# Two transformer blocks on one core: split weights in slots 4224 bytes apart, tiles of six projections moved 112 bytes in

## The chip, the cores and the metric

The kernel runs on one NeuronCore of a Trainium2 chip. The metric is the device time of one execution in microseconds (us). The clock granted to TensorE is 1.00 of its full 2.4 GHz in all stretches that are shown.

## The reference

Two blocks are applied to 256 tokens of width 2048, all in fp32. The first has a mixer of two attentions (one over 8 heads with a top-64 selection through an indexer, one over 8 heads with a gate), a cross-attention to 256 memory tokens and a SwiGLU of width 5632. The second has an adaptive modulation, an mLSTM in both directions beside a Fourier mixing, and a gated feed-forward with a convolution over the tokens. Cut to the products that matter here:

```python
proj = x @ w_in                      # q_dsa, c_kv, q_idx, k_idx, w_idx, q_m, k_m, v_m, ga, gb
o = jnp.einsum('shc,hcd->shd', o_lat, w_uv)
merged = g_a * (o_a @ w_o_dsa) + g_b * (o_b @ w_o_moba); y = merged @ w_out
k, v = jnp.split(mem @ w_kv, 2, axis=-1)
g, u = jnp.split(x @ w_in, 2, axis=-1); y = (silu(g) * u) @ w_out
p = h @ w_in                         # u_f (fourier), q, k, v, o_gate, gates
x = x + gate1[:, None, :] * (mix @ w_out)
u = depthwise_conv_centred(h2 @ w_up, w_conv, b_conv); x = x + gate2[:, None, :] * ((silu(a) * v) @ w_down)
```

## The kernel before, in words

All weights come from memory in one stream of tiles of 128 x 2048 fp32 (1 MB each), in the order of the table TILES, through four buffers `raw`. Each tile has two halves of 1024 columns. To keep fp32 accuracy with the fast format fp32r, each half is split: ScalarE copies it, rounded, to a slot of `whi` (line 633), and VectorE writes the difference `raw - whi` to the slot of `wlo` of the same number (line 1249). There are four slots in each, used in turn (`h % 4` for half h). Tokens are split in the same way: `xhi`, `xlo` (the normed input of a projection), `ohi`, `olo` (attention outputs), `mhi`, `mlo` (memory), `shi`, `slo`, `dhi`, `dlo` (sources of the wide products). A product is three matmuls: upper by upper, upper by lower, lower by upper.

A matmul on this engine first loads a block of 128 columns into the array (PEld in the profile), and then streams the other operand through it (PE). The kernel has three kinds:

- Kind (a), form "T" in `product` (line 2215): a 128x128 block of weights is loaded, and 256 tokens are streamed. The output has its features on the partitions. It serves most projections: q_idx, w_uk, qk, gate_a, gates, k_mem, q_mem, up1, lstm_q, lstm_gates, lstm_k, lstm_o, up2.
- Kind (b), in `wide_tile` (line 2258) and the turns before and after it (lines 2283, 2305): 128 tokens are loaded, 512 columns of weights are streamed. It serves out1, o_mem, down1, out2, down2.
- Kind (c), form "N" in `product` (line 2219): the same shape as (b), for the six projections whose result is wanted with tokens on the partitions: latent (three blocks of 336 columns to a half), v_moba, w_uv, v_mem, lstm_v and fourier (two blocks of 512 columns to a half).

The places in SBUF are given out by hand, in bytes of a partition. `raw` begins at 16,512, `whi` at 49,280, `wlo` at 65,664, `xhi` at 82,048, `xlo` at 98,688. The tokens do not begin at the start of `xhi` and `xlo`: the table SKEW moves them in by 112 bytes, and `behind()` puts those in `ohi`, `olo`, `mhi`, `mlo`, `ckhi` and `cklo` 16 bytes ahead of a multiple of 128, which is the same place modulo 128. Modulo 1024, `xhi`, `ohi`, `olo`, `mhi`, `mlo` begin at 240 and `xlo` at 496. The sources of the wide products, `shi`, `slo`, `dhi` and `dlo`, begin at 128 modulo 1024, and so does each slot of `whi` and `wlo`.

The order of the work on each engine is written out in the program. It is set by semaphores: TensorE waits for `lo_ready` ahead of each half tile, ScalarE for `weights_used` ahead of each slot that it writes again.

Of the kernel before, what the change touches and what calls it, by code (L numbers as in the profile page):

```python
# [6 lines left out]
F32 = mybir.dt.float32  # L7
F32R = mybir.dt.float32r
BF16 = mybir.dt.bfloat16
I32 = mybir.dt.int32  # L10
ALU = mybir.AluOpType
ACT = mybir.ActivationFunctionType
AX_X = mybir.AxisListType.X

P = 128
# [27 lines left out]
SKEW = [(112,)] * 6  # L43
# [13 lines left out]
def blocks_of(x, n, b):  # L57
# [5 lines left out]
TILES = [("latent", 3), ("q_idx", 8), ("v_moba", 8), ("w_uk", 1), ("w_uv", 1),  # L63
         ("qk", 24), ("gate_a", 16), ("gates", 32), ("out1", 16), ("k_mem", 4), ("q_mem", 4), ("v_mem", 4), ("o_mem", 4), ("up1", 8 * FC), ("down1", FT),
         ("lstm_q", 4), ("lstm_gates", 1), ("lstm_k", 4), ("lstm_v", 8), ("lstm_o", 8), ("fourier", 8), ("out2", 16),
         ("up2", 8 * FC), ("down2", FT)]
# [20 lines left out]
AT, G = starts(TILES)  # L87
# [8 lines left out]
FEW = LATENT + IDX_DIM + IDX_HEADS  # L96
BLOCKS = [(0, 0, 0, 256, 0), (0, 1, 128, 256, 256), (1, 0, 0, 128, 384), (1, 1, 0, 256, 512)]


class Order:  # L100


# [23 lines left out]
def two_blocks(nc, x, xt, memt, stream, w_ada, cols, ln_cols, rows, ln_g, ln_b, norm_f, c_row, gate_bias, dft, out, max_store, gate_store):  # L126
    with ExitStack() as ctx:
# [5 lines left out]
        def sb(name, shape, dt=F32, offset=None):  # L133

            here = place[0] if offset is None else offset
            if offset is None:
                size = int(np.prod(shape[1:])) * (2 if dt == BF16 else 4)
                place[0] += -(-size // 32) * 32
            return nc.alloc_sbuf_tensor_at(name, shape, dt, offset=here)


        raw = [sb(f"raw{s}", [P, D]) for s in range(4)]
        whi = sb("whi", [P, 4, 1024], F32R)
        wlo = sb("wlo", [P, 4, 1024], F32R)
        at_shi = place[0]
        at_xhi = place[0]
        xhi = sb("xhi", [P, KT * S + 128 // 4], F32R)
# [66 lines left out]
        at_end = place[0]  # L214
        place[0] += 4096
        ident = sb("ident", [P, P])
        ones = sb("ones", [P, P])
        warm = sb("warm", [P, P], BF16)
        dist = sb("dist", [P, 384])
        causal = sb("causal", [P, 384])  # L220
# [107 lines left out]
        hi_ready = sem("hi_ready")  # L328
        lo_ready = sem("lo_ready")
# [280 lines left out]
        def _(act):  # L610
# [8 lines left out]
            def upper(g, i=None, per=0, halves=(0, 1), slot_of=None):  # L619

                if g >= G:
                    return
                for half in halves:
                    h = 2 * g + half
                    if g < 3 and half == 0 and i is None:
                        act.wait_ge(first_half_landed[g], 16)
                    elif g < 3 or half == 0:
                        act.wait_ge(raw_landed[g % 4], at(16 * (g // 4 + 1), i, 4 * per))
                    if slot_of is not None:
                        act.wait_ge(weights_used, 2 * slot_of + half + 1)  # L630
                    elif h >= 4:
                        act.wait_ge(weights_used, at(h - 3, i, 2 * per))
                    act.activation(whi[:, h % 4], raw[g % 4][:, 1024 * half:1024 * half + 1024], ACT.Copy)\  # L633
                       .then_inc(hi_ready, 1)

            def x_first_upper(b):
# [66 lines left out]
            def second_upper_of_next(g):  # L703

                act.wait_ge(weights_used, 2 * (g - 4) + 5)
                act.activation(whi[:, (2 * g + 1) % 4], raw[g % 4][:, 1024:2048], ACT.Copy).then_inc(hi_ready, 1)

            def first_uppers(n, scale, shift):

# [53 lines left out]
            g0 = AT["latent"]  # L763
            def first_tile_upper(k):

                return act.activation(whi[:, 0, FEW * k:FEW * k + FEW], raw[0][:, FEW * k:FEW * k + FEW], ACT.Copy)

            x_first_upper(0)
            act.wait_ge(first_half_landed[0], 16)
# [37 lines left out]
            for n in range(8):  # L807
                g = AT["v_moba"] + n
# [10 lines left out]
            g = AT["w_uk"]  # L819
# [3 lines left out]
            g = AT["w_uv"]  # L823
# [13 lines left out]
            for head in range(HEADS):  # L837
                g, q = g0 + 2 * head, head % 4
# [31 lines left out]
            with act.Fori(0, 2) as i:  # L870
                for unit in range(2):
                    g, c = g0 + 8 * unit, c0 + 3 * unit
# [52 lines left out]
            def last_turn(name, src, n0, hi=shi):  # L925

                last = AT[name] + SIZE[name] - 1

                def source(s):

                    act.activation(hi[:, s], src[:, 4 * n0 + s], ACT.Copy).then_inc(shi_ready, 1)

                def half_of_more(s, half):

                    g = last - 3 + s
                    act.wait_ge(raw_landed[g % 4], 16 * (g // 4 + 1))
                    return act.activation(more_hi[name][:, 2 * (s - 1) + half], raw[g % 4][:, 1024 * half:1024 * half + 1024], ACT.Copy)

                def half_of_last(half):

                    act.wait_ge(raw_landed[last % 4], 16 * (last // 4 + 1))
                    act.wait_ge(weights_used, 2 * (last - 4) + half + 1)
                    return act.activation(whi[:, (2 * last + half) % 4], raw[last % 4][:, 1024 * half:1024 * half + 1024], ACT.Copy)

                source(0)
                if name == "down1":
                    act.wait_ge(ada_used, ADA)
                half_of_more(1, 0).then_inc(ahead_hi, 1)
                source(1)
                half_of_more(2, 0).then_inc(ahead_hi, 1)  # L950
                source(2)
                half_of_last(0).then_inc(ahead_hi, 1)
                act.wait_ge(weights_used, through(last - 4))
                source(3)
                half_of_more(1, 1).then_inc(hi_ready, 2)
                half_of_more(2, 1).then_inc(hi_ready, 2)
                half_of_last(1).then_inc(hi_ready, 2)
# [163 lines left out]
            for n in range(4):  # L1121
                name = "lstm_o" if n < 2 else "fourier"
# [116 lines left out]
        def _(dve):  # L1239
            order = Order(dve, dve_order)  # L1240

            def rest(g, i=None, per=0, halves=(0, 1)):

                if g >= G:
                    return
                for half in halves:
                    h = 2 * g + half
                    dve.wait_ge(hi_ready, at(h + 1, i, 2 * per))
                    dve.tensor_tensor(wlo[:, h % 4], raw[g % 4][:, 1024 * half:1024 * half + 1024], whi[:, h % 4].bitcast(F32),  # L1249
                                      ALU.subtract).then_inc(lo_ready, 1)  # L1250

            def x_first_rest(b):

# [62 lines left out]
            g0, wide_n = AT["latent"], LATENT + IDX_DIM + IDX_HEADS  # L1316
            def first_tile_rest(k):

                return dve.tensor_tensor(wlo[:, 0, FEW * k:FEW * k + FEW], raw[0][:, FEW * k:FEW * k + FEW],
                                         whi[:, 0, FEW * k:FEW * k + FEW].bitcast(F32), ALU.subtract)  # L1320

            x_first_rest(0)
            dve.wait_ge(first_tile_hi, 1)
# [123 lines left out]
            with dve.Fori(0, 2) as i:  # L1447
                order.enter(i, 24)
                for q in range(4):
                    g = g0 + 2 * q  # L1450
# [73 lines left out]
            def last_turn(name, src, n0, hi=shi, lo=slo):  # L1524

                last = AT[name] + SIZE[name] - 1
                turns_before = 3 * ("down1", "out2", "down2").index(name)

                def source(s):

                    dve.wait_ge(shi_ready, SRC[name] + 4 * n0 + s + 1)
                    dve.tensor_tensor(lo[:, s], src[:, 4 * n0 + s], hi[:, s].bitcast(F32), ALU.subtract).then_inc(slo_ready, 1)

                def half_of_more(s, half):

                    b = 2 * (s - 1) + half
                    return dve.tensor_tensor(more_lo[:, b], raw[(last - 3 + s) % 4][:, 1024 * half:1024 * half + 1024],
                                             more_hi[name][:, b].bitcast(F32), ALU.subtract)

                def half_of_last(half):  # L1540

                    b = (2 * last + half) % 4
                    return dve.tensor_tensor(wlo[:, b], raw[last % 4][:, 1024 * half:1024 * half + 1024], whi[:, b].bitcast(F32),
                                             ALU.subtract)

                source(0)
                dve.wait_ge(ahead_hi, turns_before + 1)
                half_of_more(1, 0).then_inc(ahead_lo, 1)
                source(1)
                dve.wait_ge(ahead_hi, turns_before + 2)  # L1550
                half_of_more(2, 0).then_inc(ahead_lo, 1)
                source(2)
                dve.wait_ge(ahead_hi, turns_before + 3)
                half_of_last(0).then_inc(ahead_lo, 1)
                source(3)
                dve.wait_ge(hi_ready, through(last - 2))
                half_of_more(1, 1).then_inc(lo_ready, 2)
                dve.wait_ge(hi_ready, through(last - 1))
                half_of_more(2, 1).then_inc(lo_ready, 2)
                dve.wait_ge(hi_ready, through(last))  # L1560
                half_of_last(1).then_inc(lo_ready, 2)

            for unit in range(4):
                g, c = AT["gates"] + 8 * unit, CH["gates"] + 3 * unit
# [438 lines left out]
            for n in range(4):  # L2003
                g = AT["lstm_o"] + 4 * n
# [134 lines left out]
        def _(pe):  # L2139
# [46 lines left out]
            def product(g, half, c, form, left, k0, ks, width, first, last, i=None, per=0, fresh=None):  # L2186
# [7 lines left out]
                    pe.wait_ge(xlo_ready, 8 * (fresh - 1) + (k0 + ks + 1) // 2)  # L2194
                if h > 0:
                    pe.wait_ge(lo_ready, at(h + 1, i, 2 * per))
                hi, lo = (w[:, h % 4, 0:ks * width].rearrange("p (k n) -> p k n", k=ks) for w in (whi, wlo))
                lhi, llo = left
                for k in range(ks):
                    kt = k0 + k  # L2200
# [559 lines left out]
```

## Time and profile before

| | us |
|---|---|
| median of 3 runs (2526.73 to 2526.83) | 2526.79 |
| the profiled execution | 2526.35 |
| its span | 2524.7 |
| TensorE busy (streams) | 2504.4 |
| TensorE busy (loads) | 2327.2 |
| VectorE busy | 1670.4 |
| ScalarE busy | 1247.2 |
| GpSimd busy | 107.6 |

How to read it: busy time is a union, so streams that overlap in their ends count once; the mean duration of a matmul contains a modelled end and is longer than the step from one start to the next. "idle before" in a group of instructions is what the engine idled just ahead of them, with what ended it. The program moved 581.95 MB by DMA, 230 GB/s on the mean.

### The profile page before, as it was taken

Reading aid. Unit: us, or ns where it says so; the run is one execution under the profiler, and the core shown is the slowest. Engines: PE = TensorE matmul, PEld = TensorE weight load, DVE = VectorE, ACT = ScalarE, POOL = GpSimd, SP = SyncE. Lnnn points to the kernel's source line nnn. Section 1 sums busy time; section 2 is a strip of 40 time slices with the busy share of each in tenths; the row PEclk is TensorE's granted clock in tenths of the full one; section 3 lists DMA queues with packets and bytes.
Section 4 is the critical chain, followed back from the end, with each engine's and each line's share of the span. In section 5 each row is a group of like instructions: output and inputs, shape, how many; then the busy total and the mean of one; then the engine's idle time right before and its main releaser. Section 6 shows DMA issues by size and latency. Waiting matters only on the chain.

```text
span 2524.7 us, 45946 instructions
## 1 busy us (share of the span) xinstructions
PE 2504.4 (99%) x17995; PEld 2327.2 (92%) x17999; DVE 1670.4 (66%) x2084; ACT 1247.2 (49%) x1588; POOL 107.6 (4%) x151
## 2 busy tenths in 40 slices
PE   9999999999999999999999999999999999999998
PEld 9799999998979999999988878988899999998886
DVE  5564675467867777777777775575766666665556
ACT  5444554444564444344444464545655555554444
POOL 0000000000100000000122000000000000000000
PEclk9999999999999999999999999999999999999999
DMA  7455445569647888888978736445455555555553
GB/s 304 154 199 186 157 146 193 187 256 362 256 157 299 332 344 329 343 330 339 363 285 330 259 135 214 167 149 216 167 187 197 193 190 199 186 196 209 190 198 118
DMA packets 82066, 581.95 MB, mean 230 GB/s; under 512 B 9308, under 2 KB 9468, under 8 KB 12096
## 3 DMA queue, kind: packets, MB, share of 16 engines
q1 hardware_dynamic: 65232, 462.98, 50.0%
q0 software_dynamic: 14464, 104.23, 10.6%
q10 hardware_dynamic: 2288, 13.59, 1.3%
q8 instruction: 58, 0.95, 0.2%
q14 instruction: 24, 0.20, 0.0%
HBM read 578.64 MB, written 2.12 MB: 230 GB/s over the span
## 4 chain that ended last, share of the span: by engine, by line
PE 96%; DVE 2%; issue 1%; ACT 1%; POOL 0%; DVEq 0%; ACTq 0%; POOLq 0%
PE ps L2215 60%; PE ps L2258 23%; PE ps L2219 7%; PE ps L2305 3%; PE ps L2283 0%; PE ps L2155 0%; PE ps L2576 0%; PE ps L2143 0%; PE ps L2417 0%; POOL small L539 0%; DVE wlo L1249 0%; PE ps L2450 0%; PE ps L2462 0%; DVE res L1838 0%; DVE res L1845 0%
## 5 line engine op out<-in xcount | busy, mean ns | idle before, releaser
L1249 DVE TENSOR_TENSOR wlo<-raw,whi 128x1024 fp32r<-128x1024 f32 x853 | 1034.0, 1227 | 659.8 <-ACT whi L633 655.9
L633 ACT ACTIVATE whi<-raw 128x1024 fp32r<-128x1024 f32 x850 | 891.3, 1060 | 961.2 <-PE ps L2215 595.0
L2215 PE MATMUL ps<-xhi,whi 128*128 128x256 f32 x4176 | 1155.4, 277 | 1.8 <-issue 1.8
L2215 PE MATMUL ps<-xhi,wlo 128*128 128x256 f32 x4176 | 1149.8, 275 | 0.0
L2215 PE MATMUL ps<-xlo,whi 128*128 128x256 f32 x4176 | 1149.6, 275 | 0.0
L2215 PEld LDWEIGHTS ps<-xhi,whi 128*128 128x128 f32 x4176 | 784.1, 188 | 4.0 <-issue 3.2
L2215 PEld LDWEIGHTS ps<-xlo,whi 128*128 128x128 f32 x4176 | 784.2, 188 | 0.4
L2215 PEld LDWEIGHTS ps<-xhi,wlo 128*128 128x128 f32 x4176 | 784.0, 188 | 0.0
L1313 DVE SCALAR_TENSOR_TENSOR ada<-ada,cb 128x2048 f32<-128x2048 f32 x96 | 219.5, 2286 | 2.7 <-DMA ada<-in_w_ada 2.7
L2258 PE MATMUL ps<-wlo,dhi 128*128 128x512 f32 x624 | 192.2, 389 | 0.0
L2258 PE MATMUL ps<-whi,dlo 128*128 128x512 f32 x624 | 192.1, 389 | 0.0
L2258 PE MATMUL ps<-whi,dhi 128*128 128x512 f32 x624 | 192.0, 389 | 0.0
L2258 PEld LDWEIGHTS ps<-whi,dlo 128*128 128x128 f32 x624 | 117.1, 188 | 24.5
L2258 PEld LDWEIGHTS ps<-wlo,dhi 128*128 128x128 f32 x624 | 117.1, 188 | 24.3
L2258 PEld LDWEIGHTS ps<-whi,dhi 128*128 128x128 f32 x624 | 117.1, 188 | 24.1
L2219 PE MATMUL ps<-whi,xhi 128*128 128x512 f32 (+1 forms) x224 | 87.9, 392 | 0.0
L2219 PE MATMUL ps<-whi,xlo 128*128 128x512 f32 (+1 forms) x224 | 85.8, 383 | 0.0
L2219 PE MATMUL ps<-wlo,xhi 128*128 128x512 f32 (+1 forms) x224 | 85.8, 383 | 0.0
L554 POOL DMA_DIRECT2D ada<-in_w_ada x94 | 50.2, 534 | 808.5 <-DVE ada L1313 790.7
L2073 DVE SCALAR_TENSOR_TENSOR conv<-ps,col,conv 128x255 f32<-128x255 f32 x176 | 72.7, 475 | 17.2 <-ACT conv L1182 17.2
L2215 PE MATMUL ps<-ohi,whi 128*128 128x256 f32 x256 | 70.6, 276 | 0.1
L2215 PE MATMUL ps<-ohi,wlo 128*128 128x256 f32 x256 | 70.4, 275 | 0.0
(374 smaller groups left out, 2179.0 us busy)
## 6 DMA issues: line engine op xcount, KB each, us to landing
raw<-in_stream SPq DMA_DIRECT2D x435, 1024.0 KB, 4.8
ada<-in_w_ada POOLq DMA_DIRECT2D x96, 1024.0 KB, 6.7
raw<-in_stream SPq DMA_DIRECT2D x5, 512.0 KB, 9.3
mem_part<-in_memt ACTq DMA_DIRECT2D x2, 1024.0 KB, 6.7
res<-in_x ACTq DMA_DIRECT2D x1, 2048.0 KB, 12.7
gamma<-in_ln_g ACTq DMA_DIRECT2D x2, 1024.0 KB, 9.8
beta<-in_ln_b ACTq DMA_DIRECT2D x2, 1024.0 KB, 14.0
gate_row<-gate_store POOLq DMA_DIRECT2D x2, 1024.0 KB, 7.7
```

Of the source, the lines that this page charges most:

```text
L554: pool.dma_start(ada[s % 2][:], w_ada[at(n0 + s, i, per)]).then_inc(ada_landed[s % 2], 16)
L633: act.activation(whi[:, h % 4], raw[g % 4][:, 1024 * half:1024 * half + 1024], ACT.Copy)\
L1249: dve.tensor_tensor(wlo[:, h % 4], raw[g % 4][:, 1024 * half:1024 * half + 1024], whi[:, h % 4].bitcast(F32), ALU.subtract).then_inc(lo_re ...
L1313: dve.scalar_tensor_tensor(out=ada[slot][:], in0=ada[slot][:], scalar=1.0, in1=cb[:], op0=ALU.mult, op1=ALU.mult, accum_out=mod[:, bass.ds ...
L2073: ins = dve.scalar_tensor_tensor(out=conv[:, q, S * m + to:S * m + to + S - 1], in0=bank[:, S * m + fro:S * m + fro + S - 1], scalar=col[: ...
L2215: ins = pe.matmul(o, w[:, k, P * m:P * m + P], a(kt), start=begins and n == 0 and m % 2 == 0, stop=ends and n == 2, skip_group_check=True)
L2219: ins = pe.matmul(o, a(kt)[:, P * m:P * m + P], w[:, k, :], start=begins and n == 0, stop=ends and n == 2, skip_group_check=True)
L2258: ins = pe.matmul(ps[:, 4 * t + 2 * half + n], a[:, s, P * t:P * t + P], w[:, h % 4, 512 * n:512 * n + 512], start=first and a is hi and w ...
L2305: return pe.matmul(ps[:, 4 * t + n], a[:, s, P * t:P * t + P], w[:, 512 * (n % 2):512 * (n % 2) + 512], start=begins and s == 0 and m == 0 ...
```

## The change

The slots of `whi` and `wlo` become 1056 columns wide (4224 bytes) instead of 1024 (4096 bytes). A new function `slot` gives the part of a slot that a half tile uses: for the six token-major projections (RESTING_TOKENS) it begins 28 columns (112 bytes) in, for all others at the start. All who write or read a half tile go through it, but for the wide products, whose tiles stay at the start of their slots. What lies behind the slots moves by 1024 bytes. `ones` shrinks from 128 to 8 columns, which gives 480 bytes back; only its first column is read.

After the change `whi` begins at 49,280 as before, `wlo` at 66,176, `xhi` at 83,072. Modulo 1024 the four slots of `whi` begin at 128, 256, 384 and 512, those of `wlo` at 640, 768, 896 and 0; all tokens begin where they did modulo 1024. The sequence of instructions and of waits is the same on every engine.

```diff
--- before.py
+++ after.py
@@ -97,6 +97,21 @@
 BLOCKS = [(0, 0, 0, 256, 0), (0, 1, 128, 256, 256), (1, 0, 0, 128, 384), (1, 1, 0, 256, 512)]
 
 
+RESTING_TOKENS = ("latent", "v_moba", "w_uv", "v_mem", "lstm_v", "fourier")
+LEVEL = SKEW[0][0] // 4
+
+
+def lane_of(g):
+
+    return LEVEL if any(AT[name] <= g < AT[name] + dict(TILES)[name] for name in RESTING_TOKENS) else 0
+
+
+def slot(w, g, half, first=0, width=1024):
+
+    first += lane_of(g)
+    return w[:, (2 * g + half) % 4, first:first + width]
+
+
 class Order:
 
 
@@ -140,8 +155,8 @@
 
 
         raw = [sb(f"raw{s}", [P, D]) for s in range(4)]
-        whi = sb("whi", [P, 4, 1024], F32R)
-        wlo = sb("wlo", [P, 4, 1024], F32R)
+        whi = sb("whi", [P, 4, 1024 + 32], F32R)
+        wlo = sb("wlo", [P, 4, 1024 + 32], F32R)
         at_shi = place[0]
         at_xhi = place[0]
         xhi = sb("xhi", [P, KT * S + 128 // 4], F32R)
@@ -214,7 +229,7 @@
         at_end = place[0]
         place[0] += 4096
         ident = sb("ident", [P, P])
-        ones = sb("ones", [P, P])
+        ones = sb("ones", [P, 8])
         warm = sb("warm", [P, P], BF16)
         dist = sb("dist", [P, 384])
         causal = sb("causal", [P, 384])
@@ -630,7 +645,7 @@
                         act.wait_ge(weights_used, 2 * slot_of + half + 1)
                     elif h >= 4:
                         act.wait_ge(weights_used, at(h - 3, i, 2 * per))
-                    act.activation(whi[:, h % 4], raw[g % 4][:, 1024 * half:1024 * half + 1024], ACT.Copy)\
+                    act.activation(slot(whi, g, half), raw[g % 4][:, 1024 * half:1024 * half + 1024], ACT.Copy)\
                        .then_inc(hi_ready, 1)
 
             def x_first_upper(b):
@@ -703,7 +718,7 @@
             def second_upper_of_next(g):
 
                 act.wait_ge(weights_used, 2 * (g - 4) + 5)
-                act.activation(whi[:, (2 * g + 1) % 4], raw[g % 4][:, 1024:2048], ACT.Copy).then_inc(hi_ready, 1)
+                act.activation(slot(whi, g, 1), raw[g % 4][:, 1024:2048], ACT.Copy).then_inc(hi_ready, 1)
 
             def first_uppers(n, scale, shift):
 
@@ -763,7 +778,7 @@
             g0 = AT["latent"]
             def first_tile_upper(k):
 
-                return act.activation(whi[:, 0, FEW * k:FEW * k + FEW], raw[0][:, FEW * k:FEW * k + FEW], ACT.Copy)
+                return act.activation(slot(whi, 0, 0, FEW * k, FEW), raw[0][:, FEW * k:FEW * k + FEW], ACT.Copy)
 
             x_first_upper(0)
             act.wait_ge(first_half_landed[0], 16)
@@ -940,7 +955,7 @@
 
                     act.wait_ge(raw_landed[last % 4], 16 * (last // 4 + 1))
                     act.wait_ge(weights_used, 2 * (last - 4) + half + 1)
-                    return act.activation(whi[:, (2 * last + half) % 4], raw[last % 4][:, 1024 * half:1024 * half + 1024], ACT.Copy)
+                    return act.activation(slot(whi, last, half), raw[last % 4][:, 1024 * half:1024 * half + 1024], ACT.Copy)
 
                 source(0)
                 if name == "down1":
@@ -1246,8 +1261,8 @@
                 for half in halves:
                     h = 2 * g + half
                     dve.wait_ge(hi_ready, at(h + 1, i, 2 * per))
-                    dve.tensor_tensor(wlo[:, h % 4], raw[g % 4][:, 1024 * half:1024 * half + 1024], whi[:, h % 4].bitcast(F32),
-                                      ALU.subtract).then_inc(lo_ready, 1)
+                    dve.tensor_tensor(slot(wlo, g, half), raw[g % 4][:, 1024 * half:1024 * half + 1024],
+                                      slot(whi, g, half).bitcast(F32), ALU.subtract).then_inc(lo_ready, 1)
 
             def x_first_rest(b):
 
@@ -1316,8 +1331,8 @@
             g0, wide_n = AT["latent"], LATENT + IDX_DIM + IDX_HEADS
             def first_tile_rest(k):
 
-                return dve.tensor_tensor(wlo[:, 0, FEW * k:FEW * k + FEW], raw[0][:, FEW * k:FEW * k + FEW],
-                                         whi[:, 0, FEW * k:FEW * k + FEW].bitcast(F32), ALU.subtract)
+                return dve.tensor_tensor(slot(wlo, 0, 0, FEW * k, FEW), raw[0][:, FEW * k:FEW * k + FEW],
+                                         slot(whi, 0, 0, FEW * k, FEW).bitcast(F32), ALU.subtract)
 
             x_first_rest(0)
             dve.wait_ge(first_tile_hi, 1)
@@ -1540,7 +1555,8 @@
                 def half_of_last(half):
 
                     b = (2 * last + half) % 4
-                    return dve.tensor_tensor(wlo[:, b], raw[last % 4][:, 1024 * half:1024 * half + 1024], whi[:, b].bitcast(F32),
+                    return dve.tensor_tensor(slot(wlo, last, half), raw[last % 4][:, 1024 * half:1024 * half + 1024],
+                                             slot(whi, last, half).bitcast(F32),
                                              ALU.subtract)
 
                 source(0)
@@ -2194,7 +2210,8 @@
                     pe.wait_ge(xlo_ready, 8 * (fresh - 1) + (k0 + ks + 1) // 2)
                 if h > 0:
                     pe.wait_ge(lo_ready, at(h + 1, i, 2 * per))
-                hi, lo = (w[:, h % 4, 0:ks * width].rearrange("p (k n) -> p k n", k=ks) for w in (whi, wlo))
+                hi, lo = (slot(w, g, half, 0, ks * width).rearrange("p (k n) -> p k n", k=ks) for w in (whi, wlo))
+                assert (lane_of(g) > 0) == (form == "N")
                 lhi, llo = left
                 for k in range(ks):
                     kt = k0 + k
```

## Rows read from the trace of the kernel before

**Rows 1.** The page of the kernel before: busy time by engine, and the last chain.

```profile
PE 2504.4 (99%) x17995; PEld 2327.2 (92%) x17999; DVE 1670.4 (66%) x2084; ACT 1247.2 (49%) x1588; POOL 107.6 (4%) x151
...
PE ps L2215 60%; PE ps L2258 23%; PE ps L2219 7%; PE ps L2305 3%; PE ps L2283 0%; PE ps L2155 0%; PE ps L2576 0%; PE ps L2143 0%; PE ps L2417 0%; POOL small L539 0%; DVE wlo L1249 0%; PE ps L2450 0%; PE ps L2462 0%; DVE res L1838 0%; DVE res L1845 0%
```

**Rows 2.** Groups by line and shape: line, engine, operation, out<-in, count, busy us, mean ns, idle before.

```profile
L2215 PE MATMUL ps<-xhi,whi 128*128 128x256 f32 x4176 | 1155.4, 277 | 1.8 <-issue 1.8
...
L1249 DVE TENSOR_TENSOR wlo<-raw,whi 128x1024 fp32r<-128x1024 f32 x853 | 1034.0, 1227 | 659.8 <-ACT whi L633 655.9
L633 ACT ACTIVATE whi<-raw 128x1024 fp32r<-128x1024 f32 x850 | 891.3, 1060 | 961.2 <-PE ps L2215 595.0 <-PE ps L2258 306.7 <-PE ps L2219 52.1
...
L2258 PE MATMUL ps<-whi,dhi 128*128 128x512 f32 x624 | 192.0, 389 | 0.0
...
L2219 PE MATMUL ps<-whi,xhi 128*128 128x512 f32 x192 | 77.5, 404 | 0.0
...
L2215 PE MATMUL ps<-ohi,whi 128*128 128x256 f32 x256 | 70.6, 276 | 0.1
...
L2258 PE MATMUL ps<-whi,shi 128*128 128x512 f32 x224 | 69.1, 390 | 0.0
...
L2219 PE MATMUL ps<-whi,mhi 128*128 128x512 f32 x32 | 13.0, 406 | 0.0
...
L2219 PE MATMUL ps<-whi,xhi 128*128 128x336 f32 x32 | 10.4, 324 | 0.0
```

**Rows 3.** Timeline, kind (a): start us, us, engine, line, operation, out<-in, count.

```profile
1900.78 0.28 PE L2215 MATMUL ps<-xlo,whi 128*128 128x256 f32 x1
...
1918.91 0.28 PE L2215 MATMUL ps<-xhi,wlo 128*128 128x256 f32 x1
```

**Rows 4.** Timeline, kind (b).

```profile
2380.95 0.62 PE L2258 MATMUL ps<-whi,dlo 128*128 128x512 f32 x2
...
2418.58 0.62 PE L2258 MATMUL ps<-wlo,dhi 128*128 128x512 f32 x2
```

**Rows 5.** Timeline, kind (c) with 512 columns.

```profile
1540.72 0.39 PE L2219 MATMUL ps<-whi,xhi 128*128 128x512 f32 x1
...
1578.99 0.39 PE L2219 MATMUL ps<-wlo,xhi 128*128 128x512 f32 x1
```

**Rows 6.** Stretches, busy us and count by engine, then granted clock, DMA share, GB/s.

```profile
1540.00:1580.00 40.00, 40.00 (x174) 32.05 (x173) 22.14 (x22) 19.71 (x21) 1.10 (x2) 1.00 0.63 223
1900.00:1940.00 40.00, 40.00 (x356) 40.00 (x355) 24.27 (x31) 22.73 (x26) 0.00 (x0) 1.00 0.55 194
2380.00:2420.00 40.00, 40.00 (x178) 33.10 (x178) 21.05 (x23) 17.55 (x23) 0.00 (x0) 1.00 0.52 184
```

**Rows 7.** Timeline, kind (a), streams (PE) and loads (PEld).

```profile
1000.04 0.28 PE L2215 MATMUL ps<-xhi,wlo 128*128 128x256 f32 x1
1000.04 0.19 PEld L2215 LDWEIGHTS ps<-xhi,whi 128*128 128x128 f32 x1
1000.15 0.28 PE L2215 MATMUL ps<-xhi,whi 128*128 128x256 f32 x1
```

**Rows 8.** Timeline, kind (c) with 336 columns.

```profile
16.95 0.31 PE L2219 MATMUL ps<-whi,xhi 128*128 128x336 f32 x1
...
17.87 0.32 PE L2219 MATMUL ps<-whi,xhi 128*128 128x336 f32 x1
...
18.79 0.31 PE L2219 MATMUL ps<-whi,xhi 128*128 128x336 f32 x1
...
19.71 0.31 PE L2219 MATMUL ps<-whi,xhi 128*128 128x336 f32 x1
```

**Rows 9.** Timeline, kind (a) after four transposes.

```profile
758.38 0.28 PE L2215 MATMUL ps<-xhi,wlo 128*128 128x256 f32 x1
...
759.56 0.28 PE L2215 MATMUL ps<-xhi,whi 128*128 128x256 f32 x1
```

**Rows 10.** Timeline, filler matmuls.

```profile
1473.35 10.83 PE L2143 MATMUL ps<-warm 128*128 128x512 bf16 x49
```

## The prediction, made before the change was run

> **What bounds the kernel now.** I read the page first. TensorE is busy 2504.4 of 2524.7 us, and four lines of matmuls hold 60 + 23 + 7 + 3 = 93% of the chain that ended last [rows 1]. So neither DMA nor VectorE (66%) nor ScalarE (49%) sets the time; the step from one matmul to the next does. Next I read the groups of instructions by shape [rows 2], for the counts. There are three kinds. (a) "Tokens stream": a 128x128 block of split weights is loaded into the array and 256 token columns stream through it, 3 x (4176 + 256 + 64) = 13,488 matmuls (the 64, of k_mem, by the code). (b) "Weights stream, wide": 128 tokens are loaded, 512 weight columns stream, 3 x (624 + 224) = 2,544 on line 2258, and by the code 432 more in the closing turns. (c) "Weights stream, token-major": the same shape on line 2219, 3 x (192 + 32) = 672 with 512 columns and 24 more of w_uv by the code, and 3 x 32 = 96 with 336. (c) is what the change aims at.
>
> A mean duration in these rows includes a modelled end and overlaps the next matmul, so I took the pace from the timeline, as the difference of two starts over the steps between them. Kind (a): 1900.78 to 1918.91 over 160 steps, 113.3 ns [rows 3]. Kind (b): 2380.95 to 2418.58 over 166 steps (84 rows of two each, the last one not counted), 226.7 ns [rows 4]. Kind (c): 1540.72 to 1578.99 over 164 steps, 233.4 ns [rows 5]. The clock is granted in full (1.00, 2.4 GHz) in all of these stretches [rows 6]. So two streams with the same number of columns, the same number of loaded columns and the same clock differ by 6.7 ns per matmul.
>
> What differs is where the bytes lie. The load of the next block starts with the stream of the present one, not after it (both at 1000.04, then 1000.15) [rows 7], so SBUF is read at two places at once. From the addresses in the code, modulo 1024: every slot of weights starts at 128; the tokens of (b) start at 128 too; the tokens of (c), and of (a), start at 240 (xhi, ohi, mhi) or 496 (xlo), 112 bytes past a multiple of 128. In (b) streamed and loaded bytes are level; in (c) the loaded tokens stand 112 bytes past the level of the streamed weights; in (a) it is the streamed tokens that do.
>
> **The change part by part.** No instruction is added, dropped or put elsewhere, and no wait changes: the sequence on each engine is the same one, and only addresses differ. Four edits:
>
> 1. Tiles of the six token-major projections start 112 bytes into their slot, level with the tokens. If the relation of the two reads makes the difference, each such matmul drops from 233.4 to 226.7 ns: (672 + 24) x 6.7 = 4.65 us. For the 96 with 336 columns no level case is in the trace. Over three steps of k they take 16.95 to 19.71, 2.76 us for 18, 153.3 ns each [rows 8]. From the level pace of kind (b), 226.7 / 512 x 336 = 148.8, a gain of 4.5 x 96 = 0.43 us. Bounds for this small part: the same 153.3 (nothing gained), or the shortest single steps there, 0.14 to 0.15 us, some 0.6 us gained. The edit together: -5.1 us, from 0 (nothing but absolute position counts) to -5.3.
>
>  Does the path take all of it? In the page the ScalarE splits wait for TensorE 961.2 us in sum [rows 2]; per half tile ScalarE needs 1060 ns and VectorE 1227 ns where TensorE of kind (c) needs 12 x 233 = 2.8 us, so a stream quicker by 3% is fed. TensorE's own idle time is 20 us in the whole span [rows 1], at the changes of stage, behind their last matmuls, so it moves with them.
>
> 2. Slots lie 4224 bytes apart instead of 4096. Modulo 1024 the slots of the upper halves now start at 128, 256, 384, 512, those of the lower halves at 640, 768, 896, 0, while all of them started at 128. Modulo 128 nothing changes for (a) and (b); modulo 256 every second slot is turned. This touches 16,464 matmuls, so it is the risk: 1 ns on each is 16 us. The trace of before has no (a) or (b) with such an offset, so I bound it. Above: kind (a) has a slower pace, for ten steps after TensorE has done something else (758.38 to 759.56, 118 ns), until it falls into its 113.3 [rows 9]; all of (a) at that pace is 4.7 x 13,488 = +63 us, and (b) at the pace of (c) +20 us. Below: the quickest stream in the trace is the filler (bf16, 512 columns, one operand), 49 in 10.83 us with a last one of 0.38, so (10.83 - 0.38) / 48 = 217.7 ns [rows 10]; half of that, 109 ns for 256 columns, is the far end, 4.4 x 13,488 = -60 us, though nothing puts kind (a) under 113.3. What I take is zero. The nearest row is the 336-column one: there the streamed weights of k = 0, 1, 2 start 0, 1344 and 2688 bytes in, so 64 bytes (k = 1) and a turned multiple of 128 (k = 2) are tried against the same tokens, and the three thirds take 0.92 us each (16.95, 17.87, 18.79, 19.71) [rows 8]. The second and third 128-multiples also occur without effect: xlo stands 256 from xhi, and blocks in a slot are 512 apart, at one pace in (a). But this is a stream-bound case with slack in the load; kind (a) has none, its loads run back to back (40.00 of 40.00 us) [rows 6].
>
> 3. ScalarE and VectorE write the splits to shifted places. At most some ns on 1060 and 1227, on engines idle a third to a half of the time. Zero; if VectorE took 10% more it would still be 1.35 of 2.7 us a half tile.
>
> 4. `ones` shrinks from 128 to 8 columns, and everything behind the slots moves by 1024 bytes or by 544. Only column 0 of it is read; its memset is at the start of GpSimd's work. Zero.
>
> Sum: 2526.35 (the profiled execution, 1.65 above its span) - 5.1 = 2521.3; the median shown is 0.44 above the profiled one, so 2521.7 on the scale of the medians.
>
> The Trainium skill speaks against this change. "TensorE: Matmul & The Clock Gate", section "Step-by-step: what each phase is for", says that TensorE reads SBUF through two ports, and that loading the next tile's weights takes no bandwidth from the running matmul; "SBUF — State Buffer" adds, under its bandwidth intuition, 16-byte lines, and 112 and 128 are multiples of 16. By that the placement is worth nothing and the time stays 2526.8. The trace is against it as far as (b) and (c) differ by 6.7 ns at one shape, but it has no pair that differs in placement alone.
>
> **The rivals.**
>
> *Every slot has to settle anew (slower).* Place: kind (a), at the change from one slot to the next. For: the slow ten steps [rows 9] show that the two reads find their best relation only gradually, and today this happens after interruptions only, since all slots look alike modulo 1024. With slots that differ, each of 13,488 / 24 = 562 half tiles may start with ten steps of 118: 562 x 10 x 4.7 ns = +26 us; with only every second one affected +13. Less the 5.1: 2535 to 2548. It decides as soon as the extra is above 9 ns per half tile of 2.72 us. Against: tokens in two positions 256 apart already alternate from matmul to matmul without a stir, and the thirds of the 336-column case are equal [rows 8].
>
> *Placement counts in itself, or not at all (no change).* The loaded tokens in (c) still start 112 past a multiple of 128, and now the weights do as well. If the cost comes from the start of the load in itself, nothing is won: 2526.8. The change then does not do what it says. For: before, (c) is the only kind whose loaded operand starts off a multiple of 128. Against: kind (a) streams from such a start, and its 113.3 is just half of the 226.7 of (b), so a start off the multiple costs the stream itself nothing.
>
> *Spread slots help the rest too (faster).* With all slots at one place modulo 1024 the reads may collide as often as they can; spread, kind (a) or (b) would lose some. A tenth of the way to 109 ns is 0.44 x 13,488 = 5.9 us, with edit 1: 2516; a fifth 2510. For: 113.3 is more than half of 217.7. Against: no row below 113 in a steady stretch.
>
> **How the numbers follow.** Edit 1 works and the rest stays: 0.42, 2521.7, its own range 2520.5 to 2523. Slots settle anew or (b) suffers: 0.27, 2530 to 2550. Nothing: 0.14. Faster than edit 1 alone: 0.17, 2505 to 2519. What tells from no change here is 0.2%, 5.05 us, and my forecast of -5.1 stands on that line: half of its chance goes to either side. Faster 0.17 + 0.22 = 0.39; same 0.14 + 0.20 = 0.34; slower 0.27. Range: 2510 (most of the faster case) to 2546 (most of the slower).
>
> **What would show it.** In the profile of after: line 2219's successors at 226.7 ns from start to start, and a mean duration near the 389 of (b) instead of 394. Kind (a) at 113.3, in all four slots; a pace that has a period of 24, 48 or 96 matmuls would be the slower rival. (b) at 226.7. Wrong would be: (c) at 233 (no effect), or a span that changed while (c) accounts for less than 4 or more than 6 us of it.

## The result

| | before | after |
|---|---|---|
| median, us | 2526.76 | 2564.38 |
| range, us | 2526.42 to 2526.83 | 2564.25 to 2564.46 |
| the profiled execution's span, us | 2524.7 | 2562.8 |

Slower by 37.6 us; the ratio is 1.0149, with a 95% interval of [1.0138, 1.0161]. The forecast was 2521.7 with a range of 2510 to 2546: wrong in sign and outside the range.

The page of the changed kernel, busy time and count by engine, to compare with [rows 1]:

```profile
PE 2543.0 (99%) x17999; PEld 2356.6 (92%) x17999; DVE 1669.9 (65%) x2084; ACT 1247.0 (49%) x1588; POOL 107.5 (4%) x151
```

TensorE is busy for 38.6 us more, with the same instructions, and the others are as they were. No wait was added: the work of TensorE itself became longer. Next the groups by line and shape (the lines have moved: 2232 is kind (a), 2275 kind (b), 2236 kind (c)), to compare with [rows 2]:

```profile
L2232 PE MATMUL ps<-xhi,whi 128*128 128x256 f32 x4176 | 1165.3, 279 | 1.8 <-issue 1.8
...
L1264 DVE TENSOR_TENSOR wlo<-raw,whi 128x1024 fp32r<-128x1024 f32 x853 | 1033.1, 1226 | 695.2 <-ACT whi L648 694.0
L648 ACT ACTIVATE whi<-raw 128x1024 fp32r<-128x1024 f32 x850 | 891.5, 1061 | 995.0 <-PE ps L2232 620.3 <-PE ps L2275 315.6 <-PE ps L2236 51.6
...
L2275 PE MATMUL ps<-whi,dhi 128*128 128x512 f32 x624 | 194.5, 392 | 0.0
...
L2236 PE MATMUL ps<-whi,xhi 128*128 128x512 f32 x192 | 77.4, 403 | 0.0
```

The splits take 1226 and 1061 ns as before (1227, 1060), and idle longer for TensorE's sake. The mean of kind (a) went from 277 to 279 ns, that of (b) from 389 to 392, that of (c) from 404 to 403. A mean with a modelled end hides most of it, so the timeline again, one stretch of kind (a) in the middle of up1, where each half tile is 24 matmuls:

```profile
989.49 0.28 PE L2232 MATMUL ps<-xhi,wlo 128*128 128x256 f32 x1
...
992.30 0.28 PE L2232 MATMUL ps<-xhi,wlo 128*128 128x256 f32 x1
...
994.45 0.28 PE L2232 MATMUL ps<-xhi,whi 128*128 128x256 f32 x1
...
995.98 0.28 PE L2232 MATMUL ps<-xlo,whi 128*128 128x256 f32 x1
```

From 989.49 to 992.30 are 24 steps of 117.1 ns, then to 994.45 are 19 of 113.2, then to 995.98 are 13 of 117.7. So the pace changes with the half tile. I then took the starts of all matmuls from the trace and sorted the steps by slot (steps above 200 ns for (a) and 300 ns for (b) left out; mean ns):

```
kind (a), 13,470 steps      slot 0   slot 1   slot 2   slot 3    all
before                      113.5    113.6    113.8    113.6    113.6
after                       114.3    117.3    114.4    117.3    115.8
kind (b), 2,540 steps       even slots        odd slots         all
before                      226.7             226.7             226.7
after                       228.0 and 229.3   232.6 and 231.6   230.4
kind (c), 512 columns, 671  (both halves)                       before 233.4, after 232.1
```

In slots 1 and 3 kind (a) never gets back to 113.3. In up1 and up2 the steps there repeat with a period of seven, rounded to ns: 118, 122, 116, 118, 116, 117, 114, a mean of 117.2. Seven is no period of the program, which has three products to a block and 24 matmuls to a half tile. In slots 0 and 2 the first three steps are slow (118, 121, 119) and the rest go at 113.4, up to the last, into the next slot, at 115. The odd slots of kind (c) have 233.2, the even ones 231.3 and 230.6: in the odd ones the 112 bytes do not make loaded and streamed bytes level, they leave them 128 bytes apart.

The account: (a) 2.2 x 13,488 = 29.7 us; (b) 3.7 x 2,544 = 9.3 us on its main line and 1.0 us in the other 432 matmuls; (c) -1.4 x 696 = -1.0 us; together 39.0 against 38.1 of span. The closing turns pay less because the middle two of their four tiles lie in buffers of their own (`more_hi`, `more_lo`), behind the slots, which moved together with the tokens. The remaining 0.9 us is in the steps that these means leave out: the long ones and those from one group to the next.

### The profile page after: what moved, and what is told of

It reads as the page before. It is cut to its first block, busy times and chain, and to the rows that moved or that the text cites. A ratio compares the mean times of both kernels' runs of the same rounds, so it can differ in the third digit from the quotient of the medians.

```text
span 2562.8 us, 45950 instructions
## 1 busy us (share of the span) xinstructions
PE 2543.0 (99%) x17999; PEld 2356.6 (92%) x17999; DVE 1669.9 (65%) x2084; ACT 1247.0 (49%) x1588; POOL 107.5 (4%) x151
## 4 chain that ended last, share of the span: by engine, by line
PE 96%; DVE 2%; issue 1%; ACT 1%; POOL 0%; DMA 0%; SPq 0%; DVEq 0%; POOLq 0%; ACTq 0%
PE ps L2232 60%; PE ps L2275 23%; PE ps L2236 7%; PE ps L2322 2%; PE ps L2300 0%; PE ps L2171 0%; PE ps L2593 0%; PE ps L2434 0%; POOL small L554 0%; DVE wlo L1264 0%; PE ps L2467 0%; PE ps L2479 0%; DMA raw<-in_stream 0%; DVE res L1854 0%; DVE res L1861 0%
## 5 line engine op out<-in xcount | busy, mean ns | idle before, releaser
L1264 DVE TENSOR_TENSOR wlo<-raw,whi 128x1024 fp32r<-128x1024 f32 x853 | 1033.1, 1226 | 695.2 <-ACT whi L648 694.0
L648 ACT ACTIVATE whi<-raw 128x1024 fp32r<-128x1024 f32 x850 | 891.5, 1061 | 995.0 <-PE ps L2232 620.3
L2275 PEld LDWEIGHTS ps<-whi,dlo 128*128 128x128 f32 x624 | 117.1, 188 | 26.9
L2275 PEld LDWEIGHTS ps<-wlo,dhi 128*128 128x128 f32 x624 | 117.1, 188 | 26.6
L2275 PEld LDWEIGHTS ps<-whi,dhi 128*128 128x128 f32 x624 | 117.1, 188 | 26.3
L2232 PE MATMUL ps<-olo,whi 128*128 128x256 f32 x256 | 71.1, 278 | 0.0
```

The lines of the kernel that those rows point to most:

```text
L648: act.activation(slot(whi, g, half), raw[g % 4][:, 1024 * half:1024 * half + 1024], ACT.Copy)\
L1264: dve.tensor_tensor(slot(wlo, g, half), raw[g % 4][:, 1024 * half:1024 * half + 1024], slot(whi, g, half).bitcast(F32), ALU.subtract).then ...
L2232: ins = pe.matmul(o, w[:, k, P * m:P * m + P], a(kt), start=begins and n == 0 and m % 2 == 0, stop=ends and n == 2, skip_group_check=True)
L2275: ins = pe.matmul(ps[:, 4 * t + 2 * half + n], a[:, s, P * t:P * t + P], w[:, h % 4, 512 * n:512 * n + 512], start=first and a is hi and w ...
```

## The experiments

All keep the sequence of instructions; only places in SBUF differ. I call the "relation" of a kind: start of what is streamed less start of what is loaded, modulo 256. Before, it is +112 in (a), 0 in (b), -112 in (c). "At level" is a relation of 0. In the changed kernel it is +112, 0 and 0 in even slots, and 128 bytes from that in odd ones. A time is followed by its ratio to the kernel before, with a 95% interval in brackets. Paces are means over the whole trace as above, in ns (for (b) on line 2258 and (c) with 512 columns, steps up to 300 ns), so for (a) the mean is 113.6 where the settled pace is 113.3. "Windows" rows have the stretch, TensorE busy us and matmuls (x), granted clock, DMA share and GB/s: the first lies in kind (a), the second in kind (b). Before had x356 and x178 there. A few matmul records can be missing from a trace, so a count is good to one or two.

**e1: the spacing alone.**

```diff
-starts (columns): 0, 1056, 2112, 3168; token-major 28, 1084, 2140, 3196
+starts (columns): 0, 1056, 2112, 3168 for all tiles
```

> Only the slot distance of 4224 bytes; the tiles of the six token-major projections start at the beginning of their slots. Theory A (slots whose start is an odd multiple of 128 stand badly to the tokens, whatever the 112 bytes do): about 2565 us, kind (a) at 113.3 ns in slots 0 and 2 after a short settling and 117.3 in slots 1 and 3, kind (b) near 230.4. Rival B (the 112 bytes do the harm, through the splits of ScalarE and VectorE or the six projections): about 2527 us.

Measured: 2563.38 us, 1.0145 [1.0128, 1.0162]. (a) 115.8, (b) 230.4, (c) 230.7 (its slots alternate between the relations -112 and +16, which have 233.4 and 228.3 below).

```profile
900.00:940.00 40.00, 40.00 (x348) 1.00 0.86 322
2380.00:2420.00 40.00, 40.00 (x175) 1.00 0.56 197
```

348 and 175 instead of 356 and 178. Theory A holds: the spacing alone costs 36.7 us of the 37.6. The rival of the 112 bytes falls. They cost about 1 us on top, where they meet the wrong spacing: kind (c) has 232.1 with them and 230.7 without, 1.4 x 696 = 1.0 us.

**e4 and e2: slots at multiples of 256 bytes, without and with the 112 bytes.** Both need no more memory than the changed kernel: the gaps are put ahead of the odd slots.

```diff
-whi slots (columns): 0, 1056, 2112, 3168; token-major 28, 1084, 2140, 3196
+whi slots (columns): 0, 1088, 2112, 3200; token-major 28, 1052, 2140, 3164   (e2; e4: as the others)
```

> The same slots at multiples of 256 bytes, without the 112 bytes. Theory A: as the kernel before, 2526.8 within 1 us, kind (c) at 233.4. Rival C: 2545 to 2560. The difference to the kernel with the 112 bytes is what the 112 bytes are worth alone: 4.6 us if kind (c) falls to 226.7.

> The same memory as the changed kernel, but every slot starts at a multiple of 256 bytes from the first one (0, 4352, 8448, 12800) for tiles of kinds (a) and (b), and at such a multiple plus 112 (112, 4208, 8560, 12656) for the six token-major projections. Theory A (the relation of the two reads counts modulo 256): kind (a) 113.3 and kind (b) 226.7 in all slots as in the kernel before, kind (c) between 226.7 and 231, and the time 2521 to 2526. Rival C (slots must be alike modulo 1024, since each change between unlike slots unsettles the reads): kind (a) with a slow start in each half tile, 2540 to 2555.

Measured: e4 2526.82 us, 1.0000 [0.9991, 1.0010]; e2 2525.21 us, 0.9994 [0.9984, 1.0003]. In e4 (a) 113.6, (b) 226.7, (c) 233.5; in e2 (a) 113.6, (b) 226.7, (c) 231.7.

```profile
900.00:940.00 40.00, 40.00 (x355) 1.00 0.88 339
2380.00:2420.00 40.00, 40.00 (x179) 1.00 0.54 189
```

```profile
900.00:940.00 40.00, 40.00 (x355) 1.00 0.89 339
2380.00:2420.00 40.00, 40.00 (x178) 1.00 0.53 185
```

The slots in e4 are as unlike modulo 1024 as 0, 256, 256, 512 bytes from the first, and nothing is lost. So unlikeness in itself does no harm (rival C falls), and a distance of 256 bytes is as good as none, where one of 128 is not (e1). It also keeps the smaller `ones` and the shift of all that lies behind the slots, so these cost nothing. The 112 bytes alone are worth 1.6 us between these two, not 4.6, and by its interval e2 can't be told from before; the trace says why the gain is small: kind (c) at a relation of 0 goes at 231.7 and not at the 226.7 that kind (b) has at the same relation.

**e3 and x: all slots turned by 128 bytes, then tokens and slots together.**

```diff
-whi slots 0, 1024, 2048, 3072           of a tensor at 49,280
+whi slots 32, 1056, 2080, 3104, wlo slots 128 bytes further too       (e3: xhi and all behind it keep their place modulo 1024)
+the same, and xhi, xlo, shi and all behind them also 128 bytes further (x)
```

> Slots 4096 bytes apart as before, all of them 128 bytes further on against the tokens, without the 112 bytes. Theory A (an odd multiple of 128 is bad in itself, also where all slots are alike): kind (a) 117.3 ns everywhere, + 4 x 13,488 = +54 us, kind (b) +4 to +6 ns on 2,976, +12 to +18 us, together 2593 to 2600 us. Rival D (only the change from slot to slot costs; a relation that stays the same settles): 2527 to 2530 us.

> Slots 4096 bytes apart and turned by 128 bytes as in e3, and everything behind them (all tokens and sources) turned by 128 bytes too, without the 112 bytes. Theory A (the relation counts): every pace as in the kernel before, 2526.7 within 1 us. Rival F (the absolute place of the slots modulo 256 counts): as e3, kind (a) 117.2, about 2586.

Measured: e3 2586.13 us, 1.0235 [1.0218, 1.0252]; x 2526.50 us, 1.0000 [0.9990, 1.0009]. In e3 (a) 117.2 in every slot, (b) 232.5, (c) 228.3; in x all three as before (113.6, 226.7, 233.4). The timeline of kind (a), first of e3 (155 steps between the two rows, 117.2 ns), then of x (160 steps, 113.3):

```profile
900.83 0.28 PE L2246 MATMUL ps<-xlo,whi 128*128 128x256 f32 x1
...
918.99 0.28 PE L2246 MATMUL ps<-xhi,whi 128*128 128x256 f32 x1
```

```profile
900.78 0.28 PE L2246 MATMUL ps<-xhi,whi 128*128 128x256 f32 x1
...
918.91 0.28 PE L2246 MATMUL ps<-xlo,whi 128*128 128x256 f32 x1
```

A relation that is the same throughout does not settle to 113.3 if it is the wrong one: rival D falls. The same absolute place of the slots with the tokens moved along costs nothing: rival F falls. What counts is the relation. The steps of kind (a) in e3 have the same period of seven as in the odd slots of the changed kernel. My sum for e3 was some 10 us too high: (a) paid 3.6 ns and not 4, (b) 5.8 on its main line and less in the closing turns, and (c) gained 5.1 x 696 = 3.6 us, which I had not expected; its relation there is 128 - 112 = +16. A rival that I did not test by itself is a clash with the writes of ScalarE and VectorE into the slots. Against it: the pattern of seven repeats all through up1 and up2.

**g1 to g4, k1, k2: other relations for (b) and (c).** Slots as in e4, tiles of (c) and of (b) moved in by their own number of bytes.

```diff
-token-major tiles at +112 bytes, wide tiles at 0
+g1 128 and 16; g4 144 and 32; k2 160 and 0; g3 176 and 64; k1 192 and 192; g2 224 and 112
```

> Slots at multiples of 256 bytes as in e2 and e4, kind (a) as before. What is streamed starts, modulo 256, 16 bytes ahead of what is loaded in kind (c) (tiles 128 bytes in) and in kind (b) (tiles 16 bytes in). Theory A (the pace of a kind is a function of this relation modulo 256): kind (c) at the 228.3 ns that it had when all slots were turned, which is the same relation, -3.6 us over its 696 matmuls; kind (b) not known, between 217.7 and 233; where kind (b) stays 226.7 the time is 2523. Rival E (what helped kind (c) in the turned kernel was the absolute place): kind (c) at 231 to 233.

> The same with a relation of +112 bytes, the one that kind (a) has, in kinds (c) (tiles 224 bytes in) and (b) (tiles 112 bytes in). Theory A in its strong form (what is best for kind (a) is best for all): kind (c) and kind (b) at or under 226.7 ns, 2521 us or less. Its weak form (each kind has its own best): kind (c) between 226 and 233, kind (b) above 226.7, some 2520 to 2545 us. Kind (a) stays at 113.3 in any case.

> Relation +64 bytes in kinds (b) and (c). Theory A: a pace of its own, between those of +16 and +112 or equal to one of them, the same in all slots and passes; the time 2515 to 2545. A pace that differs by slot would speak against a period of 256.

> Relation +32 bytes in kinds (b) and (c). As for +64: a pace between its neighbours, the time 2515 to 2545.

> As best_plus64, with kind (c) at a relation of +48. Theory A: kind (a) 113.3, kind (b) 226.7, kind (c) a pace of its own between 226 and 233.4; 2521.5 to 2526.8.

> Kind (c) at a relation of +80, kind (b) at +192 (that is -64). Theory A: kind (a) 113.3; kind (c) between 226 and 233.4; kind (b) between 226.7 and 233.5, so 2521 to 2546. Should kind (b) mirror (+64 gave it 228.9), it gives 2526 to 2532.

Measured, mean step in ns by relation (kind (a) stays at 113.6 in all six):

```
relation   -112    -64      0    +16    +32    +48    +64    +80   +112   +128
kind (b)      -  233.3  226.7  231.7  233.3      -  228.9      -  231.1  232.5
kind (c)  233.4      -  231.7  228.3  232.6  232.2  226.9  230.2  233.2  233.2
```

(0 of (b), -112, 0 and +16 of (c) are those of before, e2 and g1; +128 of (b) is that of e3. +128 of (c) is read from the odd slots of the changed kernel, where each half tile of 12 comes from a slot with another relation.)

Times: g1 2536.82 us, 1.0040 [1.0026, 1.0054]; g2 2538.62, 1.0047 [1.0031, 1.0064]; g3 2530.06 (2528.35 to 2533.07, the widest of all, which I can't explain; its trace is that of the quickest execution, so 228.9 for (b) at +64 is a low value), 1.0014 [1.0004, 1.0023]; g4 2544.35, 1.0070 [1.0053, 1.0087]; k2 2525.77, 0.9997 [0.9987, 1.0006]; k1 2542.32, 1.0062 [1.0047, 1.0077]. Kind (b) in g4, 78 steps between these two rows, 233.3 ns; before it was 226.7 [rows 4]:

```profile
2384.73 0.63 PE L2290 MATMUL ps<-wlo,dhi 128*128 128x512 f32 x2
...
2402.93 0.40 PE L2290 MATMUL ps<-wlo,dhi 128*128 128x512 f32 x1
```

Kind (c) has 228.3 in g1 as in e3, at the same relation, so rival E gains nothing; but the streamed bytes stand at the same absolute place in both, so it is x, not g1, that excludes the absolute place. The strong form of theory A in g2 falls: +112, the better of the two relations that (a) was run at (+112 and -16), is near the worst for (c). Other relations for (a), which has most of the matmuls, were not tried. The pace is no smooth function of the relation: +48 and +64, 16 bytes apart, give 232.2 and 226.9. A mirror for (b), +64 against -64, there is not (228.9, 233.3).

**best: (a) and (b) left, (c) at +64.**

```diff
-token-major tiles at columns 28, 1052, 2140, 3164   (e2)
+token-major tiles at columns 44, 1068, 2156, 3180   (176 bytes in)
```

> Slots at multiples of 256 bytes; kind (a) as before (relation +112), kind (b) as before (relation 0), the tiles of kind (c) 176 bytes in, a relation of +64 modulo 256. Theory A adds up the paces measured so far: kind (a) 113.3, kind (b) 226.7, kind (c) 226.9 instead of 233.4, so 6.5 ns x 696 = 4.5 us less: 2522.1. If the kinds disturb each other where they meet: 2523 to 2528.

Measured: 2522.13 us (2521.88 to 2522.46), 0.9983 [0.9974, 0.9992], 4.5 us under before, as the sum of paces had it. (a) 113.6, (b) 226.7, (c) 226.9. Kind (c) in its timeline, 44 steps between the rows, 226.8 ns, where before had 233.4 [rows 5]:

```profile
1549.81 0.39 PE L2251 MATMUL ps<-whi,xlo 128*128 128x512 f32 x1
...
1559.79 0.39 PE L2251 MATMUL ps<-whi,xhi 128*128 128x512 f32 x1
```

## Why the prediction was wrong

- The reading of what bounds the kernel held: the loss is in the step between matmuls, and the change added no wait. The sum of paces over counts, made before that run, gave the time of the best kernel to 0.1 us.
- The step that failed is the second edit, "What I take is zero". The distance of 4224 turned every second slot by 128 bytes against the tokens, and this cost 29.7 us in (a) and 10.3 in (b) (e1 shows it alone, e4 its absence). The bounds that I had set from rows, +63 and +20 us, held even for a turn of all slots: e3 has 48 and 16. The evidence that I set against them, the three equal thirds of the 336-column case [rows 8], did not bear: kind (c) with 336 columns had a mean between 153.1 and 155.4 ns in every run, whatever its relation (by thirds 151.4 to 155.2, but for one of 159.6 in g4), so it hardly sees the effect. With 512 columns the same kind has 233.4 and 228.3 at two of the three relations that those thirds have, -112 and +16. The pairs 256 and 512 bytes apart [rows 3] were sound, but they speak of multiples of 256 only. That was the gap in the trace of before, named there, and then priced by the likeliest guess.
- The slower rival had the right edit and kind, and a wrong course. It let the reads settle after ten steps; in fact in odd slots they don't settle at all (117.3 as the mean of all 24), and in even slots they do after three. It gave +13 to +26 us, (b) aside; kind (a) paid 29.7. Its 2535 to 2548 is 16 us short of the 2564.38.
- The first edit was mis-sized: 1.4 ns and 1.0 us in the changed kernel, where only the even slots are level, 1.7 ns and 1.6 us alone (e2 less e4), instead of 6.7 ns and 4.65 us. I took the pace of (b) at level for the pace of (c) at level. e2 and g1 show that kinds (b) and (c) have different paces at one relation: 226.7 and 231.7 at 0, 231.7 and 228.3 at +16. The gain that I forecast is there, but at +64. For the 336 columns I had 0.43 us; nothing came (153.4 before, 153.6 after).
- The third and fourth edits cost nothing, as said: the splits took 1226 and 1061 ns, and e4, which keeps the fourth edit, took as long as before.
- The Trainium skill, "TensorE: Matmul & The Clock Gate", section "Step-by-step: what each phase is for", has it that the load of the next weights takes no SBUF read bandwidth from the running matmul. The conclusion that I drew from it, that placement is worth nothing, is refuted by e3 and x: with the same instructions, 128 bytes between loaded and streamed bytes are 3.6 ns on 113.6 and 5.8 on 226.7. The measurement decides. Whether what is lost is read bandwidth, no run here shows.
- The Trainium skill, "SBUF — State Buffer", section "Door 1: The DMA port swizzle" (and not the one on bandwidth that the prediction names), has lines of 16 bytes, with a price for going from one to the next. They do not explain it, as all of these places are multiples of 16, and +48 and +64 differ by 5.3 ns in (c).

What stays open: why (b) and (c) differ at one relation. One difference is the order of the loads. (c) loads another block for each matmul, and goes to and fro between `xhi` and `xlo`; (b) on line 2258 loads the same block four times and the next twice. At level this alone does not seem to be it: the closing turns (line 2305) load another block for two matmuls in three for most of their length, and their steps in the trace of before have 226.7 as well, with the same mean duration as line 2258 [rows 2]:

```profile
L2305 PE MATMUL ps<-wlo,dhi 128*128 128x512 f32 x32 | 12.1, 389 | 0.0
```

Away from level the order isn't excluded. Nor does a matmul's own relation give its pace where neighbours have another: in g3 the matmuls of the middle two tiles of the closing turns, at level, took 231.0 ns between those at +64, and not 226.7. A second difference is that the tokens of (c) start 112 bytes past a multiple of 128 and those of (b) at one; I ran no kernel with both places moved by 112. What mechanism makes the pattern, I can't say.

## What to carry to other kernels

When TensorE is bound by back-to-back matmuls, the distance in SBUF between what it streams and what it loads is part of the kernel: a change of a buffer's pitch should keep it modulo 256 bytes for each kind of matmul, or be measured. Read the step between starts for each kind and buffer slot, not the mean duration. A placement found good for one kind need not be good for another, and a stretch that doesn't react to placement can't vouch for one that does.

## What the runs showed of the hardware

- fp32r matmuls, 128x128 loaded and 256 columns streamed: 113.3 ns a step at one relation (+112), 117.2 at 128 bytes from it (-16), both at a granted clock of 1.00. With 512 columns between 226.7 and 233.4 ns, over seven relations in (b) and nine in (c).
- The relation counts modulo 256 bytes: slots that differ by 256 (e4) behave alike, slots that differ by 128 (e1) don't. Moving both operands by 128 (x) changes nothing.
- In (a) at -16 the steps repeat with a period of seven (114 to 122 ns, mean 117.2), without end (after, e3); at +112 three slower steps come first after a turned slot, ten after transposes [rows 9].
